# Splitting the last three tiles' tail in a hybrid attention, convolution and expert-retrieval block

## What is computed

```
h = rms_norm(x, g0) * (1 + scale1) + shift1
y = hybrid_mixer(h)        # attention + convolution branches, sigmoid gates from h @ w_in, then @ w_out
x = x + gate1 * rms_norm(y, g1)
h = rms_norm(x, g2) * (1 + scale2) + shift2
q = h @ w_q                # 8 heads, two halves of 128
s1, s2 = q1 . keys1, q2 . keys2            # 128 keys each
top 16 of each, then top 16 of the 256 sums -> expert number, softmax gate
pre = x_row . expert_down[expert]          # 128 experts per token, rows of 2048
y   = sum over experts of gelu(pre) * gate * expert_up[expert]
x = x + gate2 * rms_norm(y, g3)
```

## Time and profile before

| | us |
|---|---|
| median of 3 runs | 4188.42 |
| the profiled execution | 4186.43 |
| its span | 4184.6 |
| PE busy | 2812.4 (67%) |
| DVE busy | 2284.2 (55%) |
| ACT busy | 541.4 (13%) |
| POOL busy | 1391.0 (33%) |
| moved by DMA | 1413.23 MB, mean 338 GB/s |

### The profile page before, as it was taken

One profiled execution on the slowest core, in us unless ns is written; L12 is line 12 of the kernel. 1 busy time (PEld: TensorE's weight loads), 2 busy tenths in 40 slices (PEclk: granted clock), 3 DMA queues, 4 the chain that ended last, 5 costly groups with the idle time before them and its releaser, 6 DMA issues.

```text
span 4184.6 us, 37663 instructions
## 1 busy us (share of the span) xinstructions
PE 2812.4 (67%) x15140; PEld 1597.2 (38%) x15140; DVE 2284.2 (55%) x3525; ACT 541.4 (13%) x1191; POOL 1391.0 (33%) x1109
## 2 busy tenths in 40 slices
PE   5899899889899999997983434434444444434435
PEld 3687788789855555553540100100101101101101
DVE  6399779742564333325674665664666664444442
ACT  2221221200210101012120100100100110000000
POOL 2421211000012333322334454434434444344342
PEclk8899999999999999998985555555555555555556
DMA  9463434798658998986879999999999999999998
GB/s 350 145 217 130 156 100 142 278 370 318 211 207 322 370 375 344 378 330 244 336 288 421 393 405 421 421 422 421 421 421 417 422 421 415 421 422 419 422 421 369
DMA packets 303725, 1413.23 MB, mean 338 GB/s; under 512 B 24384, under 2 KB 24512, under 8 KB 167104
## 3 DMA queue, kind: packets, MB, share of 16 engines
q0 software_dynamic: 152064, 1107.36, 64.4%
q1 hardware_dynamic: 145568, 291.53, 19.7%
q10 hardware_dynamic: 5920, 11.94, 0.8%
HBM read 1403.35 MB, written 7.39 MB: 337 GB/s over the span
## 4 chain that ended last, share of the span: by engine, by line
PE 41%; DMA 38%; DVE 13%; POOL 3%; issue 3%; ACT 2%; SPq 0%; DVEq 0%; ACTq 0%; POOLq 0%
PE psum L608 41%; DMA front<-in_down,back 30%; DMA front<-in_up,back 5%; DVE front L1607 4%; POOL front L579 3%; DVE back L1375 2%; DMA front<-in_w_in 2%; DMA back<-in_ada_w 1%; DVE back L1344 1%; ACT back L1137 1%; POOL x_low L563 0%; DVE back L1708 0%; ACT front L1241 0%; DVE back L1442 0%; DVE w_low L1330 0%
## 5 line engine op out<-in xcount | busy, mean ns | idle before, releaser
L608 PE MATMUL psum<-front 128*32 128x512 f32 (+2 forms) x6608 | 1401.8, 662 | 934.5 <-DMA front<-in_up,back 851.6
L1607 DVE CUSTOM_DVE_ANT_0 front<-front,back 128x2048 f32<-128x2048 f32 x512 | 1171.2, 2292 | 1357.3 <-DMA front<-in_down,back 1230.0
L608 PEld LDWEIGHTS psum<-front 128*32 128x32 f32 (+1 forms) x6608 | 573.5, 161 | 1697.6 <-issue 1430.1
L579 POOL DMA_INDIRECT front<-in_down,back x512 | 596.9, 1166 | 913.8 <-DVE back L1607 666.6
L579 POOL DMA_INDIRECT front<-in_up,back x442 | 515.4, 1166 | 1003.3 <-PE psum L608 951.7
L608 PE MATMUL psum<-back,front 128*32 128x128 f32 (+3 forms) x4400 | 631.5, 453 | 312.7 <-DMA back<-in_up,back 174.5
L608 PEld LDWEIGHTS psum<-back,front 128*32 128x32 f32 (+1 forms) x4400 | 368.4, 166 | 582.1 <-issue 328.2
L557 POOL TENSOR_TENSOR w_low<-front,w_high 128x2048 fp32r<-128x2048 f32 x33 | 156.0, 4728 | 551.2 <-ACT w_high L1025 551.2
L608 PE MATMUL psum<-x_high,w_high 128*128 128x512 f32 x640 | 253.2, 396 | 7.8 <-POOL x_low L563 4.7
L608 PE MATMUL psum<-x_high,w_low 128*128 128x512 f32 x640 | 251.2, 393 | 0.0
L608 PE MATMUL psum<-x_low,w_high 128*128 128x512 f32 x640 | 251.1, 392 | 0.0
(11 more groups left out here) (161 smaller groups left out, 1686.0 us busy)
## 6 DMA issues: line engine op xcount, KB each, us to landing
front<-in_w_in SPq DMA_DIRECT2D x116, 1024.0 KB, 7.4
back<-in_ada_w SPq DMA_DIRECT2D x64, 1024.0 KB, 9.0
front<-in_ada_w POOLq DMA_DIRECT2D x32, 1024.0 KB, 9.5
front<-in_w_out SPq DMA_DIRECT2D x32, 1024.0 KB, 6.3
front<-in_w_q SPq DMA_DIRECT2D x32, 1024.0 KB, 5.3
front<-in_w_conv_o SPq DMA_DIRECT2D x16, 1024.0 KB, 7.5
front<-in_w_attn_o SPq DMA_DIRECT2D x16, 512.0 KB, 9.3
front<-in_down,back POOLq DMA_INDIRECT x512, 17.2
```

The source lines that it names most:

```text
L579: nc.gpsimd.indirect_dma_start(out=row_, out_offset=None, in_=table[:, :], in_offset=bass.IndirectOffsetOnAxis(ap=idx4[:, t % 2, c:c + 1], ...
L608: return nc.tensor.matmul(o, a, b, start=start, stop=stop)
L1607: V.tensor_tensor_reduce(d_row[s], d_row[s], h2r, 1.0, 0.0, ALU.mult, ALU.add, pre[:, b // 16 % 2, b % 16:b % 16 + 1]).then_inc(dots_done, 1)
```

## The change

The tail of tiles 1 to 3 is cut in two behind the mixing. The stages are now: mixing of tile 0; rest of tile 0; mixing of tiles 1 to 3 (384 columns); rest of tile 1 (`w_out`, `x`, `w_q`, scores and routing with 128 columns); rest of tiles 2 and 3 (256 columns). Retrieval begins beside the third stage, as before, and runs beside three stages.

```
-TAIL = ((0, P), (P, S - P))
+STAGES = (("mix", 0, P), ("rest", 0, P), ("mix", P, S - P), ("rest", P, P), ("rest", 2 * P, S - 2 * P))
-WIDE = 160
+WIDE = 208
 def block_pace():
-    return [(i + 1) * 128 // tail_chunks(1) for i in range(tail_chunks(1))]
+    out = [(i + 1) * 100 // 48 for i in range(48)] + [101 + i for i in range(16)] + [118]
+    out += [120, 123, 126, 128] + [128 + 8 * min(i, 2) for i in (1, 2, 3) for _ in range(4)]
+    out += [144 + 3 * (i + 1) // 2 for i in range(16)] + [172, 176]
+    out += [176 + 3 * (i + 1) // 2 for i in range(16)]
-D_KB, U_KB = (64, 72, 80, 0, 8), (88, 96, 104, 16, 169)
-D_SLOT = slot_table(BLOCKS, WIDE, 3, len(D_KB))
-U_SLOT = slot_table(BLOCKS, WIDE, 3, len(U_KB))
+D_KB, U_KB = (64, 72, 80, 160, 0, 8), (88, 96, 104, 16, 169)
+D_SLOT = slot_table(BLOCKS, (0, 3), (128, 4), (WIDE, len(D_KB)))
+U_SLOT = slot_table(BLOCKS, (0, 3), (WIDE, len(U_KB)))
-        sc = [view(kb, KT, P) for kb in (169, 144, 152, 160)]
+        sc = [view(kb, KT, P) for kb in (169, 144, 152, 144)]
```

The rest of the diff follows from it or moves small steps. On TensorE the scores of a query group now stand before the last chunk's `retrieve`, and the retrieval at `x` behind the squares:

```
-                        chunk_out(c)
+                    if s < chunks - 1 or behind is None:
+                        chunk_out()
+                if behind is not None:
+                    behind()
+                    chunk_out()
```

(`behind` is the function with the scores.) On ScalarE the exponential of the last routing group stands at the end of its own stage, ahead of the copy of `g3r`, and the retrieval at `x` behind the second square root:

```
-                    if c == 1 and cg == 0:
-                        gate_exp(0, 3)
...
-                    passed(c, 1)
+                    passed(1)
                     if i:
-                        gate_exp(c, i - 1)
-                if c == 0:
+                        gate_exp(r, i - 1)
+                gate_exp(r, 3)
+
+            for c, (kind, _, _) in enumerate(STAGES):
+                if c == FIRST:
                     act.wait_ge(g3_done, 1)
                     A(g3r, ps[:, 7, :], ACT.Copy).then_inc(g3_ready, 1)
```

Tile 2's routing moves from slices between the dots of blocks 156 and up into the last stage, behind each query group; only tile 3's stays in slices:

```
-                    if 2 <= t < TT and b % 128 >= 28 and n < 4:
+                    if t == TT - 1 and b % 128 >= 28 and n < 4:
```

More of the change, by code:

```diff
@@ L81, in tail_counts @@
     d = a = v = 0
[L82 to L86, removed]
+    for c in range(len(STAGES)):
+        for kind, i, _ in tail_groups(c):
             done[c, kind, i], act[c, kind, i], dve[c, kind, i] = d, a, v
@@ L102, in chunk_ends @@
     out, plain = [], 0
[L103 to L106, removed]
+    for c in range(len(STAGES)):
+        for kind, i, k in tail_groups(c):
             for _ in range(k - 1):
@@ L519, in _ @@
             nc.sync.dma_start(keys[0].rearrange("p k c -> p (k c)"), keysT).then_inc(keys_in, 16)
[L520 to L547, removed]
@@ L888, in chunk_in, with chunk_out @@
                 return s
-            def chunk_out(c):
+            def chunk_out():
                 nonlocal chunk_at
                 chunk_at += 1
[L893 to L915, removed]
-                        chunk_out(c)
-                def plain(k):
-                    return k
-                def squares(buf, count, first, last):
-                    for i in range(count):
-                        ins = mm(ps[:, 6, 0:n], ones, buf[:, i, 0:n], first and i == 0, last and i == count - 1)
-                    return ins
@@ new lines, in chunk_out, with group @@
+                retrieve(reached(chunk_at))
+            def group(chunks, per, src, place, t0, n, free, base, between=None, behind=None):
+                for s in range(chunks):
+                    r = tring[chunk_in()]
+                    for m in range(4):
+                        if s == 0 and free is not None:
+                            pe.wait_ge(free, base + m + 1)
+                        for k in range(per):
+                            ins = mm(ps[:, m, 0:n], r[:, k, m * P:(m + 1) * P], src[:, place(per * s + k), t0:t0 + n],
+                                     s == 0 and k == 0, s == chunks - 1 and k == per - 1)
+                        if s == chunks - 1:
+                            ins.then_inc(g_done, 1)
+                    if s < chunks - 1:
+                        ins.then_inc(t_used, 1)
+                    if s == 0 and between is not None:
+                        between()
+                    if s < chunks - 1 or behind is None:
+                        chunk_out()
+                if behind is not None:
+                    behind()
+                    chunk_out()
@@ L949, in tail, with rest, squares @@
                         modulation_columns(2)
+            def rest(c):
+                nonlocal chunk_at
+                (_, t0, n), r = STAGES[c], NTH[c]
+                def squares(buf, count, first, last):
+                    for i in range(count):
+                        ins = mm(ps[:, 6, 0:n], ones, buf[:, i, 0:n], first and i == 0, last and i == count - 1)
+                    return ins
                 for i in range(4):
@@ L993, in _ @@
-            tail(0)
-            g3_rows()
-            tail(1)
+                        group(4, 4, hT, plain, t0, n, act_took, ATOOK[c, "sc", i - 1], None, scores)
+            for c, (kind, _, _) in enumerate(STAGES):
+                if c == FIRST:
+                    g3_rows()
+                if kind == "mix":
+                    mix(c)
+                else:
+                    rest(c)
             retrieve(END)
```

227 lines of the change are left out of this document (144 added, 83 removed).

## The result

The changed kernel took 4220.76 us (median of 4 runs, 4216.06 to 4223.2) against 4190.32 us for the kernel before on the same chip: ratio 1.0077, 95% interval 1.0062 to 1.0092. So it is slower, as forecast, but by 30 us, where 80 were forecast. The time lies in the lower half of the forecast range (4182 to 4330); the size of the change was forecast more than twice too large.

The account below looks back on a forecast made before the run. Bound by DMA bytes from 2190 us, by PE beside the tail before. Added DMA work +93 us, idle time 177 to 164 (-13), gives +80: 4186.4 becomes 4266 profiled, 4268 us median; range 4182 to 4330.

Parts of the forecast that it names:

- What bounds the kernel: From 1156 to 2190 us PE is busy nearly all the time; from 2190 us on the DMA engines are full.
- the end moves by as much as dot 200: Behind dot 200, starting at 2557 us before, 312 blocks run unchanged at full DMA; buffer count makes no difference; shift 80 us.
- The start: Up to the first dot: dots start near 1190 instead of 1211, PE stalls some 10 us, 25 us DMA idle.
- Mixing: 100 blocks over 48 chunks, PE and DMA equally full, 25 us idle (bounds 5 and 70), ending near 1800.
- The `x` of tile 1: Tile 1's `x` stage: three buffers of each kind cover most of the chain, 8 us idle, ending near 1956.
- the new hole: Tile 1's query groups: down gathers from block 128 wait for routing, 76 us DMA idle (bounds 45 and 100).
- 15 + 18 + some 6: Wait at blocks 136 and 144: chunks and scores, routing, issue and landing; 39 us, 9 filled by chunk loads, 30 idle each.
- 93 us for the added loads: Reading `w_out` and `w_q` once more: 32 chunks of 1 MB at 2.92 us each of DMA work.
- the prediction's other bound: Lower bound on the added chunk loads, if a chunk costs no more than a gather's bytes: 32 x 2.52 = 81 us.
- The last stages: Tiles 2 and 3 up to dot 200: `w_out` 4, `x` 10, query 12 us idle; bounds 10 and 60 together.
- A: Rival: loads and prefetched gathers fill every routing wait, mixing keeps DMA full; idle 70, faster below 84, 4174 us; chance 0.13.
- B: Rival: PE's clock falls to half in the narrow stages behind mixing, +55 us over the forecast, 4323 us; chance 0.17.

Follow-up runs that it names:

- the two quarter runs: The changed kernel with only the first quarter of tile 1's weight chunks loaded: `w_out` and `w_q` together, 4189.77 us; `w_q` alone, 4217.74 us.

## Why the prediction was wrong

**Right.** What bounds the kernel, and the direction. That the end moves by as much as dot 200 held in number (33 and 31 us), in part by luck: it was to follow from the same work in the same time behind dot 200, with three buffers as good as five, and there a lead of 6 gathers and a loss of 12 us at block 224 made up for each other. The start: the first dot at 1189.5 (forecast near 1190), with TensorE 9.53 us behind `g3r` (forecast some 10):

```profile
1176.87 1.93 PE L634 MATMUL psum<-back,front 128*32 128x128 f32 x32 [9.53 <-ACT front L1302]
...
1189.52 2.29 DVE L1650 CUSTOM_DVE_ANT_0 front<-front,back 128x2048 f32<-128x2048 f32 x1
```

Mixing: 100 dots at 1798 (forecast 1800), 24 us idle (25), PE 564 of 610 us. The `x` of tile 1: 5 idle (8).

**The step that failed: "the new hole", 76 us idle, with "15 + 18 + some 6" us at the second and third borders.** The three stretches without a dot are there, 26, 32 and 54 us from one dot's start to the next, and GpSimd waits for the routing's last step (L1628) as said. The issues of the down gathers 128, 136 and 144, and the dots around them:

```profile
2014.76 0.94 POOL L605 DMA_INDIRECT front<-in_down,back  x1 [29.48 <-DVE back L1628]
...
2082.47 0.94 POOL L605 DMA_INDIRECT front<-in_down,back  x1 [35.44 <-DVE back L1628]
...
2150.43 0.94 POOL L605 DMA_INDIRECT front<-in_down,back  x1 [35.78 <-DVE back L1628]
```

```profile
1994.47 2.29 DVE L1650 CUSTOM_DVE_ANT_0 front<-front,back 128x2048 f32<-128x2048 f32 x1 [4.19 <-DMA front<-in_down,back]
2020.26 2.29 DVE L1650 CUSTOM_DVE_ANT_0 front<-front,back 128x2048 f32<-128x2048 f32 x1 [5.77 <-DMA front<-in_down,back]
...
2056.39 2.29 DVE L1650 CUSTOM_DVE_ANT_0 back<-back 128x2048 f32<-128x2048 f32 x1 [2.88 <-DMA back<-in_down,back]
2064.40 0.87 DVE L1573 MAX8 back<-back 128x8 f32<-128x128 f32 x4 [5.71 <-ACT back L1292]
...
2087.89 2.29 DVE L1650 CUSTOM_DVE_ANT_0 front<-front,back 128x2048 f32<-128x2048 f32 x1 [2.39 <-DMA front<-in_down,back]
...
2124.23 2.29 DVE L1650 CUSTOM_DVE_ANT_0 back<-back 128x2048 f32<-128x2048 f32 x1 [3.10 <-DMA back<-in_down,back]
...
2177.80 2.29 DVE L1650 CUSTOM_DVE_ANT_0 front<-front,back 128x2048 f32<-128x2048 f32 x1
```

Two things differ. VectorE waited only 5.7 us for the second group's scores (2064.40), where I had 15: TensorE's last up rows come before VectorE's last dots, so its three chunks run beside the last two dots (2046 to 2062 below) and not behind them. And a GpSimd queue that stands for 36 us is not an idle DMA engine. The windows ahead of and inside the second stretch, and inside the third:

```profile
2046.00:2062.00 16.00, 13.17 (x96) 11.54 (x97) 6.99 (x7) 1.09 (x4) 0.94 (x1) 0.76 0.95 361
2062.00:2086.00 24.00, 7.51 (x67) 5.88 (x65) 20.05 (x92) 5.94 (x22) 2.81 (x3) 0.76 0.45 161
2118.00:2150.00 32.00, 32.00 (x258) 31.35 (x255) 21.52 (x78) 4.24 (x18) 0.00 (x0) 0.94 0.86 311
```

In 2118 to 2150 TensorE is busy all 32 us: the fourth group has no blocks in its pace, so the chunks of the third and the fourth run through in one go, and SP reloads the three buffers (from 2139 on with the next stage's `w_out`) as fast as TensorE empties them, 311 GB/s with no gather issued. I had allowed each stretch three chunk loads, the number of buffers, where the right count is the chunks that TensorE passes in it. Idle was 18 + 14 + 5 = 37 us and not 76; forecast was 16 + 30 + 30, so it is the second and third border that failed. By bytes it is 43 us (74.9 MB in the 226 us from 1952 on, at 409 GB/s), so this does not hang on how idle time is read. The runs without routing (-23 us) and with the pace that covers it (-17 us) fit that size and not 76.

**The second term mis-sized: 93 us for the added loads.** The ledger has 76 us more DMA work. The price of 2.92 us per chunk was read in a stretch that TensorE bounds, where the share says how long packets were under way, and not what they would take if the engines were full. In the full window of tile 1's `w_out` the engines move 409 GB/s with the weights among them; by that 33.6 MB are 82 us, and the prediction's other bound, 81 us, was nearer. (The 76 us are no clean price either: they hold the 6 gathers that the changed kernel is ahead, and the kernel before's work is read at shares of 0.77 to 0.91, which the last section shows to be too high a reading.) And by the two quarter runs the loads are not one price: 28 us (31 - 3) for 12.6 MB where the DMA engines are full, 3 us for 12.6 MB in the stretch of the routing waits. The Trainium skill ("DMA: Bandwidth & Descriptors", Specifications) with its 435 GB/s would have given an estimated 77 us; the fullest stage window with weights here (1800 to 1919) shows 409.

**Sum**, by the share. The hole is 39 us less than forecast, the loads 17 less, small terms 6 less. The last stages are 13 more: `w_out`, `x` and queries of tiles 2 and 3 were 2 + 13 + 24 idle (4 + 10 + 12 forecast). So 80 becomes 31.

**Rivals.** A (the holes fill) had the right mechanism in half: they fill by half, to 37 us, and the whole idle time to 132, over the 84 from which it would have won. B (the clock falls): PEclk did fall, to 0.68 and 0.65 in the first two windows of the queries, and was 0.85 at `w_out`, where the stage was at full DMA share with TensorE busy 81 of 119 us. Where TensorE had work in one piece (2118:2150) it had 0.94. The Trainium skill's case ("TensorE: Matmul & The Clock Gate", HAM oscillation) is seen in that 0.85, where 128-column chunks wait for full DMA engines. The 55 us of B did not come. Whether a smaller part of the queries' time is owed to the clock, say in the scores that VectorE waited 5.7 us for, no run tested.

## What to carry to other kernels

When work is moved into a stretch with slack, keep a ledger of the resource that bounds the rest: added work minus idle time saved, stage by stage. Price the added transfers by the rate in a full stretch, and do not charge a wait as idle before looking at what other queues will do in it: here half of the added loads lay in the new waits and cost next to nothing. A split that makes stages narrow moves them from one bound to another, so the pace must be shifted with it, and no border between tiles should fall into a chain. When buffers grow later than before, look at which periodic wait they now meet while they are few.

## What the runs showed of the hardware that was not expected

The mean busy share of the DMA engines is not a rate. At 0.90 the kernel before moved 351 GB/s in mixing, which is 390 at a share of 1. The changed kernel moves 409 GB/s at 1.02 (1800 to 1919), which is 401, with a larger part of weights in it. The rows of the two queues say the same, in the window 1958:2190 of the kernel before, then 1190:1800 and 1800:1919 of the changed one:

```profile
q0 software_dynamic: 7391, 53.87, 59.2%
q1 hardware_dynamic: 7056, 13.89, 17.2%
...
q0 software_dynamic: 25527, 185.94, 75.0%
q1 hardware_dynamic: 23877, 47.95, 21.2%
...
q0 software_dynamic: 4561, 33.24, 67.9%
q1 hardware_dynamic: 7384, 15.31, 34.0%
```

A MB of weights takes 2.87, 2.70 and 2.64 us, at shares of 0.77, 0.96 and 1.02; with the 2.78 of the prediction at 0.90 the order is the same. A MB of gathered rows takes 2.55, 2.46 and 2.43 us. So packets take longer by this count in the stretches where the engines have gaps; why is open. Idle time read as (1 - share) is therefore too small in a stretch that is not full, and prices per MB read there are too high: 2.92 us per chunk where the full window has 2.77 by its own row, and 2.56 by the 409 GB/s of all its bytes.
